# A mixture-of-experts stage: gather and combination as two rounded products with an exact 0/1 table, and the last weight piece loaded during the routing

## The reference

```
aff = softmax(h2 @ w_router)                 # 512 x 16
gval, idx = top_k(aff.T, 64)                 # each expert takes its 64 best tokens
xe  = h2[idx]                                # gather
hid = silu(xe @ w_gate[e]) * (xe @ w_up[e])  # 1024 -> 1024
ye  = (hid @ w_down[e]) * gval
out[idx] += ye                               # combination
```

## Time and profile before

| | us |
|---|---|
| median of 3 timed runs (lowest, highest) | 3082.7 (3081.36, 3086.76) |
| profiled execution | 3083.14 |
| its span, first to last instruction | 3081.3 |
| PE busy | 2980.7 (97%) |
| DVE busy | 1659.1 (54%) |
| ACT busy | 1190.9 (39%) |
| POOL busy | 963.2 (31%) |
| DMA queue q1 | 435.29 MB, 35.9% of 16 engines' span |

### The profile page before, as it was taken

One profiled execution on the slowest core, in us unless ns is written; L12 is line 12 of the kernel. 1 busy time (PEld: TensorE's weight loads), 2 busy tenths in 40 slices (PEclk: granted clock), 3 DMA queues, 4 the chain that ended last, 5 costly groups with the idle time before them and its releaser, 6 DMA issues.

```text
span 3081.3 us, 58082 instructions
## 1 busy us (share of the span) xinstructions
PE 2980.7 (97%) x24214; PEld 2523.1 (82%) x24214; DVE 1659.1 (54%) x2706; ACT 1190.9 (39%) x2273; POOL 963.2 (31%) x685
## 2 busy tenths in 40 slices
PE   7999899999999989999999999999999999999998
PEld 5678788544444449999998999999999999889996
DVE  4257755532212246847384558456676455477583
ACT  3154423110000035535524546346454443364453
POOL 1030367100000024233564432344332366343322
PEclk9999999989999999999999999999999999999999
DMA  7531100359999962322221122222332222113321
GB/s 305 222 129 55 70 3 3 139 214 427 429 429 429 429 264 75 110 83 103 81 99 55 56 97 101 92 103 76 109 110 76 97 83 83 56 69 110 110 78 53
DMA packets 38227, 440.07 MB, mean 143 GB/s; under 512 B 6104, under 2 KB 6744, under 8 KB 11994
## 3 DMA queue, kind: packets, MB, share of 16 engines
q1 hardware_dynamic: 36536, 435.29, 35.9%
q10 hardware_dynamic: 1448, 1.31, 0.1%
HBM read 433.69 MB, written 2.11 MB: 141 GB/s over the span
## 4 chain that ended last, share of the span: by engine, by line
PE 58%; DVE 2%; ACT 2%; issue 1%; POOL 0%; DVEq 0%; ACTq 0%
PE PS L3065 23%; PE PS L2933 23%; PE PS L2930 4%; PE PS L2944 2%; PE PS L3466 2%; PE PS L2521 1%; PE PS L3501 1%; PE PS L2527 1%; PE PS L3484 1%; ACT w_hi L2862 1%; DVE t_lo L3036 0%; ACT h_hi L2743 0%; PE PS L2534 0%; ACT low L2746 0%; PE PS L3461 0%
## 5 line engine op out<-in xcount | busy, mean ns | idle before, releaser
L2875 POOL TENSOR_TENSOR w_lo<-low,w_hi 128x512 fp32r<-128x512 f32 (+4 forms) x310 | 629.0, 2035 | 1522.0 <-ACT w_hi L2862 1517.1
L2862 ACT ACTIVATE w_hi<-low 128x512 fp32r<-128x512 f32 (+3 forms) x670 | 485.3, 743 | 475.4 <-PE PS L2933 290.0
L3065 PE MATMUL PS<-t_hi,w_hi 128*128 128x264 f32 (+1 forms) x1152 | 327.1, 284 | 7.8 <-ACT low L3139 7.8
L3065 PE MATMUL PS<-t_hi,w_lo 128*128 128x264 f32 (+1 forms) x1152 | 327.5, 284 | 0.0
L3065 PE MATMUL PS<-t_lo,w_hi 128*128 128x264 f32 (+1 forms) x1152 | 326.2, 283 | 0.0
L2880 DVE TENSOR_TENSOR w_lo<-low,w_hi 128x512 fp32r<-128x512 f32 x360 | 258.6, 735 | 31.8 <-ACT w_hi L2862 30.5
L3065 PE MATMUL PS<-h_hi,w_lo 128*128 128x264 f32 (+1 forms) x864 | 244.9, 283 | 0.0
L3065 PE MATMUL PS<-h_hi,w_hi 128*128 128x264 f32 (+1 forms) x864 | 244.5, 283 | 0.4 <-issue 0.4
L3065 PE MATMUL PS<-h_lo,w_hi 128*128 128x264 f32 (+1 forms) x864 | 244.8, 283 | 0.0
L2933 PE MATMUL PS<-g_hi,w_hi 128*128 128x264 f32 x1056 | 230.8, 286 | 1.2 <-DVE high L3327 1.2
L2933 PE MATMUL PS<-g_lo,w_hi 128*128 128x264 f32 x1056 | 228.6, 284 | 0.0
(11 more groups left out here) (474 smaller groups left out, 6688.4 us busy)
## 6 DMA issues: line engine op xcount, KB each, us to landing
arena<-wts_dram SPq DMA_DIRECT2D x101, 2048.0 KB, 18.7
low<-wts_dram SPq DMA_DIRECT2D x77, 2048.0 KB, 7.8
arena<-wmod_dram SPq DMA_DIRECT2D x9, 2048.0 KB, 9.0
low<-wts_dram SPq DMA_DIRECT2D x12, 1536.0 KB, 6.4
arena<-na_bias_dram SPq DMA_DIRECT2D x16, 512.0 KB, 3.7
high<-tab_dram SPq DMA_DIRECT2D x1, 2225.0 KB, 25.6
arena<-x_cols_dram SPq DMA_DIRECT2D x1, 2048.0 KB, 8.7
arena<-x_dram SPq DMA_DIRECT2D x1, 2048.0 KB, 8.2
```

Of the source, the lines that this page charges most:

```text
L2862: nc.scalar.activation(hi, raw, ACT.Copy).then_inc(w_h.sem, 1)
L2875: nc.gpsimd.tensor_tensor(lo, raw, hi.bitcast(F32), ALU.subtract).then_inc(w_lp.sem, 1)
L3065: last = nc.tensor.matmul(PS[:, b, 0:n], wt[wi][:, k, :], xs[xi], start=(i in (0, 1, 3) and k == 0 and j == 0), stop=(k == 3 and j == 2), ...
```

## The change

Exact fp32 products with the table are replaced by two rounded ones. A value h is split into h_hi (rounded to fp32r by ACT) and h_lo = h - h_hi (DVE, rounded on writing). The table holds 0 and 1, which fp32r holds exactly, so table x h_hi + table x h_lo gives h up to the rounding of h_lo.

- Gather: `h2` is split in the routing (`split_high` on ACT, `split_low` on DVE). 64 rounded products take the place of 32 fp32 ones. `onehot` is a small rounded table for one pair now, and DVE builds that of the next pair (`next_onehot`) when the gather of the present one is over. The large table (L2280) goes.
- Combination: the table must be 0/1, so the affinity moves into the scaling of `ye`. DVE takes from the transposed weighted table the maximum of each row (`slot_aff`) and the comparison `> 0` (`wcur`, rounded). `ye` is scaled by both `slot_aff` and GT2, ACT rounds it, DVE makes the difference. 16 rounded products take the place of 8 fp32 ones, and four banks (0, 1, 6, 7) take the place of two.
- Last weight piece: the ring gets 95 pieces. Piece 95 (the second half of the last "down") is loaded in two halves of 1 MB into spare room at the end of SP's list of the routing. The DMAs of `meta`, `ln_in` and `final_norm` wait for the last "down", because they write where a half of the piece lies.
- Table 1 is put in another order, so that some of its room is free.

```diff
+            sp.wait_ge(ss_done, TT)
+            sp.wait_ge(h2_done, TT)
+            sp.dma_start(spare[1], last[:, 1, :, :]).then_inc(spare_in, 16)
+            sp.wait_ge(lt_ps, TT)
+            sp.dma_start(spare[0], last[:, 0, :, :]).then_inc(spare_in, 16)
...
+    def split_high(act, n):
+        act.wait_ge(h2_done, n + 1)
+        nc.scalar.activation(h2_hi[:, YORD[n], :], h2[:, YORD[n], :], ACT.Copy).then_inc(hh, 1)
+    def split_low(dve, n):
+        dve.wait_ge(hh, n + 1)
+        dve.wait_ge(ht_ps, 2 * n + 2)
+        nc.vector.tensor_tensor(h2_lo[:, YORD[n], :], h2[:, YORD[n], :], h2_hi[:, YORD[n], :].bitcast(F32), ALU.subtract).then_inc(h_lo, 1)
...
             for n in range(3):          # ACT, routing
                 squares(n)
                 deviation(n)
+                if n == 1:
+                    split_high(act, 0)
+                    split_high(act, 1)
             turned(0)
             turned(1)
+            split_high(act, 2)
...
             turned(3)
+            split_high(act, 3)
             logits(3)
...
             for n in range(TT):         # DVE, routing
                 added(n)
                 normed(n)
+                if n == 2:
+                    split_low(dve, 0)
+                    split_low(dve, 1)
             nc.vector.memset(affT[0:NE, :], 1.0)
+            split_low(dve, 2)
+            split_low(dve, 3)
             dve.wait_ge(lg_ps, 1)
...
+            with sp.Fori(1, NP - 1) as i:
+                load_pair(i, 2 * RING)
+            load_pair(NP - 1, 2 * RING - 1)
...
+            sp.wait_ge(ye_ps, 2 * NP)
             sp.dma_start(res[:, :, 0:NMETA], A["meta"].rearrange("p (k n) -> p k n", k=DK)).then_inc(in_ld, 16)
...
             def gather(i):
                 for k in range(DK):
-                    for t in range(TT):
-                        last = nc.tensor.matmul(..., h2[:, t, k * P:(k + 1) * P],
-                                                onehot[:, t, bass.ds(2 * CAP * i, 2 * CAP)], start=(t == 0), stop=(t == TT - 1))
+                    for x, part in enumerate((h2_hi, h2_lo)):
+                        for t in range(TT):
+                            last = nc.tensor.matmul(..., part[:, t, k * P:(k + 1) * P],
+                                                    onehot[:, t, :], start=(x == 0 and t == 0), stop=(x == 1 and t == TT - 1))
...
             def combine(i):
-                pe.wait_ge(ye_sb, 2 * i + 2)
+                pe.wait_ge(yl_sb, 2 * i + 2)
...
-                    nc.tensor.matmul(PS[:, c % 2, :], wcur[:, t * P:(t + 1) * P], ye[:, half * 512:(half + 1) * 512],
-                                     start=True, stop=True).then_inc(cb_ps, 1)
+                    for x, part in enumerate((ye_hi, ye_lo)):
+                        last = nc.tensor.matmul(PS[:, CBANK[c % 4], :], wcur[:, t * P:(t + 1) * P], part[:, half * 512:(half + 1) * 512],
+                                                start=(x == 0), stop=(x == 1))
+                    last.then_inc(cb_ps, 1)
...
+                for half in range(2):   # ACT, end of pair(i)
+                    act.wait_ge(ye_sb, 2 * i + (half + 1))
+                    nc.scalar.activation(ye_hi[:, lo:hi], ye[:, lo:hi], ACT.Copy).then_inc(yh_sb, 1)
...
             def turned_weights(i):
                 dve.wait_ge(wt_ps, i + 1)
-                nc.vector.tensor_copy(wcur, PS[:, 2, :]).then_inc(wc_sb, 1)
+                nc.vector.reduce_max(slot_aff, PS[:, 2, :], AX.X)
+                nc.vector.tensor_scalar(wcur, PS[:, 2, :], 0.0, None, ALU.is_gt).then_inc(wc_sb, 1)
+                nc.vector.drain()
+            def next_onehot(i):
+                dve.wait_ge(xe_ps, 2 * i + 2)
+                dve.wait_ge(ow_sb, i + 1)
+                for t in range(TT):
+                    last = nc.vector.tensor_tensor(heads(onehot[:, t, :], 2), over(C["iota"], 2), spread(codet[:, t, bass.ds(2 * i + 2, 2)], CAP),
+                                                   ALU.is_equal)
+                last.then_inc(oh_sb, 1)
...
-                    nc.vector.tensor_tensor(ye[:, lo:hi], PS[:, 6 + half, :], GT2[:, lo:hi], ALU.mult).then_inc(ye_sb, 1)
+                    nc.vector.scalar_tensor_tensor(ye[:, lo:hi], PS[:, 6 + half, :], slot_aff, GT2[:, lo:hi], ALU.mult, ALU.mult).then_inc(ye_sb, 1)
+                for half in range(2):
+                    dve.wait_ge(yh_sb, 2 * i + (half + 1))
+                    nc.vector.tensor_tensor(ye_lo[:, lo:hi], ye[:, lo:hi], ye_hi[:, lo:hi].bitcast(F32), ALU.subtract).then_inc(yl_sb, 1)
```

More of the change, by code:

```diff
@@ L2161, in down @@
                         if k % 4 == 0:
-                            w = chunk(i, 8 + 2 * half + k // 4)
+                            if final and half == 1 and k:
+                                pe.wait_ge(spare_in, 32)
+                                w = spare
+                            else:
+                                both = chunk(i, 8 + 2 * half + k // 4)
+                                w = [both[:, j, :, :] for j in range(2)]
                             if half == 0:
@@ L2165, in down @@
                         for j, (a, b) in enumerate(OWN):
-                            last = nc.tensor.matmul(PS[a:b, 6 + half, :], hidT[:, k, j * CAP:(j + 1) * CAP], w[:, j, k % 4, :],
+                            last = nc.tensor.matmul(PS[a:b, 6 + half, :], hidT[:, k, j * CAP:(j + 1) * CAP], w[j][:, k % 4, :],
                                                     start=(k == 0), stop=(k == DK - 1))
@@ L2175, in pair @@
                 gate_up(i, 1)
+                if not isinstance(i, int) or i:
+                    pe.wait_ge(cb_sb, 8 * i + 4)
                 if not last:
-                    if not isinstance(i, int) or i:
-                        pe.wait_ge(cb_sb, 8 * i + 2)
-                    else:
-                        pe.wait_ge(oh_sb, 1)
+                    pe.wait_ge(oh_sb, i + 1)
                     gather(i + 1)
@@ L2183, in pair @@
                 turn_weights(i)
-                down(i)
+                down(i, last)
             gather(0)
@@ L2255, in combined @@
                     x = x1[:, t, half * 512:(half + 1) * 512]
-                    nc.vector.tensor_tensor(x, x, PS[:, c % 2, :], ALU.add).then_inc(cb_sb, 1)
+                    nc.vector.tensor_tensor(x, x, PS[:, CBANK[c % 4], :], ALU.add).then_inc(cb_sb, 1)
             def pair(i, last=False):
                 own_weights(i)
+                if not last:
+                    next_onehot(i)
                 for j in range(2):
@@ L2275, in pair @@
                     lo, hi = half * 512, (half + 1) * 512
-                    nc.vector.tensor_tensor(ye[:, lo:hi], PS[:, 6 + half, :], GT2[:, lo:hi], ALU.mult).then_inc(ye_sb, 1)
-            nc.vector.drain().then_inc(cb_sb, 2)
-            for t in range(TT):
-                last = nc.vector.tensor_tensor(heads(onehot[:, t, 2 * CAP:], NE - 2), over(C["iota"], NE - 2), spread(codet[:, t, 2:], CAP),
-                                               ALU.is_equal)
-            last.then_inc(oh_sb, 1)
+                    nc.vector.scalar_tensor_tensor(ye[:, lo:hi], PS[:, 6 + half, :], slot_aff, GT2[:, lo:hi], ALU.mult, ALU.mult).then_inc(ye_sb, 1)
+                for half in range(2):
+                    dve.wait_ge(yh_sb, 2 * i + (half + 1))
+                    lo, hi = half * 512, (half + 1) * 512
+                    nc.vector.tensor_tensor(ye_lo[:, lo:hi], ye[:, lo:hi], ye_hi[:, lo:hi].bitcast(F32), ALU.subtract).then_inc(yl_sb, 1)
+            nc.vector.drain().then_inc(cb_sb, 4)
             first_rows(0)
```

59 lines of the change are left out of this document (39 added, 20 removed).

## The result

| | before | after |
|---|---|---|
| median of 11 timed runs (lowest, highest) | 3084.33 (3081.36, 3086.76) | 3089.42 (3084.37, 3095.16) |
| ratio after/before, 95% interval | | 1.0019 [1.0011, 1.0026] |
| span of the profiled execution | 3081.3 | 3088.0 |
| code transposes to second block's first matmul | 482.1 | 487.5 |

The kernel became about 5 us slower, against a forecast of 1.9 us faster. The last row is what I compare throughout: it starts at the routing's code transposes (648.13 before, 648.63 after), just ahead of gather(0). Profiles of one kernel against another differ by several us before that point, in the first block, which the change doesn't touch.

The account below looks back on a forecast made before the run. The weight stream (58.8 us a pair at 428 GB/s) was taken to bound the stage. Tail with last piece -1.7 and stream start -0.2 gave -1.9 us: 3083.14 to 3081.2, median 3080.8, stated as 3081.0, range 3077.3 to 3085.

Parts of the forecast that it names:

- Start of the stream (b): gather(0), just ahead of the weight stream: 9.01 us, partly at 1.2 GHz, would get 0.6 us shorter with cheaper records.
- T: The experiments' theory, not the prediction's: loss is PE's clock, left at 1.2 GHz by rounded 128-column records in the first gather.
- rival 1: A rounded 128-column product costs as much as an fp32 one: gather 14.8 us, pairs PE-bound, 3117 us; chance 0.05.
- Rival 4: The clock falls in PE's new gaps inside the stage; two slow pieces in the last pair, 3088 us; chance 0.04.
- Gather: Per pair on PE: 64 rounded records at 0.105 us, 6.9 us in all, 0.5 less than before.
- rival 2: The rounded weight load is faster: gather 4.1 us, gather(0) gains 4.0 instead of 0.6, 3077.6 us; chance 0.05.
- Savings inside the stage worth nothing: In the pairs: PE would need 53.9 us against the stream's 58.8, so it would only wait some 4.9 us more.
- Routing: Ahead of the stream: splitting h2 mostly fits idle time of ACT and DVE, delaying the softmax by 0.4 us.
- Last piece: End of the stream: with one piece preloaded, down ends at 1110.1 instead of 1111.55, a gain of 1.45 us.
- Tail: From down to the second block: 2.2 us scaling and rounding before a faster combination; second block 1.7 us earlier, last piece included.
- rival 3: SP's wait for the last down delays ln_in and final_norm, features(0) at 1139: +15 us, 3098; chance 0.03.
- rival 5: The weight stream is not the bound, so up to 29 us come free in the pairs, 3054 us; chance 0.03.

Follow-up runs that it names:

- cold_wide: wide without the 15 dummy products (results unread) that keep PE at work during the routing's top-64 search; 1.0007 of before, gather(0) 9.9 us.
- nospare: The changed kernel with the last weight piece back in the ring, 96 pieces in the stream; 1.0020 of before.
- cold_narrow: The changed kernel without the 15 dummy products that keep PE at work during the routing's top-64 search; 1.0028 of before, gather(0) 13.8 us.
- t23: The changed kernel with two dummy products of 512 columns ahead of the last combination and three behind it; 1.0013 of before.
- w2: The changed kernel with two fp32 dummy products of 512 columns on PE behind the routing's code transposes; 0.9998 of before, gather(0) 7.3 us.
- slow: w2 with three dummy products of 512 columns on PE behind each pair's combination; 0.9996 of before.
- early: w2 with the first weight piece's products moved between k-tiles 4 and 5 of gather(0); 1.0001 of before.
- wide: The changed kernel with 48 of gather(0)'s 64 rounded products moving 256 columns instead of 128; 0.9998 of before, gather(0) 7.5 us.
- g0: The changed kernel with gather(0) alone as 32 fp32 products of the rounded part, low part left out; 0.9994 of before.
- bw2: The kernel before with the same two dummy products behind the code transposes as w2; 1.0002 of before.
- best1: w2 with the dummy products of t23 around the last combination; 0.9999 of before.
- best2: wide with the dummy products of t23 around the last combination; 0.9995 of before.

## Why the prediction was wrong

**The step that failed** is "Start of the stream (b)": "With 0.105 instead of 0.115 per record, doubled in the slow part, -0.6." It took the slow part of gather(0) as given, as long as it had been (650.6 to 654.0), and only re-priced the records in it. But how long it lasted changed with the records. In after the clock was down for 17 us, from 651.1 to 668.1, over the rest of the gather and on into the first piece. In place of -0.6 the profile showed +4.6 for gather(0) and +1.9 for piece 0; with the routing's 0.5 the stream started 7.0 us later. Two of the prediction's own signs of being wrong came with it: records further than 0.18 us apart (0.212), and a clock under 1.00 inside the stage.

What the clock did with each kind of product, where the profiles show it: it came back during the fp32 gather (before, 3.7 us in) and during the one with 256 columns (cold_wide, 5.3 us in). During the rounded gather with 128 columns it didn't (after, nospare, cold_narrow), and once it fell (t23). The timed runs bear out both comparisons, w2 with after and cold_wide with cold_narrow. The idea behind T, that what counts is for how long columns move behind each load, is not shown: the runs compare two widths only. And the rounded gather doesn't always lose the clock when it starts with it: in w2, slow, early and best1, with the dummies right ahead, it ran at 1.00 to its end.

The prediction's bounds for the record gave "-3.6 and +9.4", and +7.0 lies inside them, but by luck: +9.4 was the price of a rounded record that costs as much as an fp32 one everywhere (rival 1), and at full clock the record cost 0.112.

**Rival 4** was the nearest, "the clock falls", but it looked for that in the gaps that the change opens in the pairs, and priced two slow pieces in the last pair. Those gaps did nothing: up to 1.24 us, clock 1.00 over the whole pair. The 5 us were lost in the densest row of the timeline, and that its 3088 comes near the measured 3089.4 is luck. New gaps did go with a low clock in the tail (2.24 and 2.66 us), which it did not price.

Step by step:

- *Combination* forecast 4.3, was 4.54. *Gather* forecast 6.9, was 7.17 (0.112 a record, not 0.105): right in kind, small misses. Rival 1 (0.232 a record) and rival 2 (0.064) are both refuted. On rival 2 the Trainium skill, "TensorE: Matmul & The Clock Gate", section "Weight-path perf modes — Fast Weight Load (FWL) and DoubleRow", has loads of 128 weights in a type other than FP32 go faster. If rounded fp32 counts as such, the runs disagree: 0.112 us a record, and in wide 1.75 times the columns for 0.24 us more. (The prediction gives what this rule would take off the sum as 3.5 us; its own rival 2 works it out to 3.4.)
- *Savings inside the stage worth nothing*: right, and shown by slow. PE waited 3.3 us a pair, not 4.9. Of the 1.6, 0.5 are the two misses of size above, 0.1 the pair of 58.7 instead of 58.8, and 0.5 that a piece behind a wait takes 3.65 where one in the flow takes 3.47 (839.29 - 825.43 in the earlier trace rows, a quarter of it), three times; the rest I did not follow.
- *Routing* forecast +0.4. The softmax moved from 629.51 to 630.02, but operations at 603 and 618, ahead of the rounding, had moved by the same 0.5, so the rounding itself cost nothing that this profile shows.
- *Last piece* forecast -1.45; nospare shows 1.4 in the stream.
- *Tail*: 2.2 us forecast between down and combination, 2.24 measured. From the end of down to the second block 18.4 were forecast; 18.1 where the clock stayed up (w2, g0, early and the three with dummies in the tail), 19.4 in after, where x1's diagonal products ran at 0.72. That is a second loss of clock, behind a wait on DVE that was 0.30 us and is now 2.66. Six of the nine profiles without dummies there had one in the tail, and neither before nor bw2 did (18.7 and 18.6); that the longer waits are the cause is likely, not shown.
- *New wait on SP*, rival 3: refuted. ln_in's issue took 0.66 us instead of 21.49.
- *Stream the bound*, rival 5: refuted, share 1.01 as before.

So the mechanism of the stage was right, and at full clock its size nearly so: w2 less bw2 is -1.8. That this is so near to -1.9 is in part luck. The forecast holds +0.4 for the routing, which the stages leave out; without it, it was -2.3 (lead -0.6, end of down -1.45, tail -0.25), against -0.1, -1.2 and -0.5 measured. From there to the measured stages: after less w2 is +7.7 in the lead, -0.3 in the stream and +1.3 in the tail, the first and the last from the clock, and bw2 less before is -1.5, before's own loss in the same place. -1.8 + 8.7 - 1.5 = 5.4 = 487.5 - 482.1.

**Open.** Why the clock is up at the start of gather(0) in some profiles (in w2, slow, early, bw2 and best1, all with the two dummies, but also in g0, wide, t23 and best2, with 1.54 us idle as in after) and down in others (before, after, nospare). Within one profile each, I can't say how often either happens; the timed medians say that after lost it often. And why 128 rounded columns behind each load leave the clock low where 256, or fp32 products, do not.

## What to carry to other kernels

Before a product is replaced by narrower or cheaper ones, look at the granted clock where it starts. Here a run of weight loads with 128 rounded columns behind each counted as busy in every row and still stayed at 1.2 GHz, and then the piece behind it paid too. When a transfer stream bounds the middle of a stage, count an engine's saving only in the lead and the tail: here the same change was worth nothing inside the pairs and went with a loss of 6.5 us in the lead. And an earlier start of a stream helps only if the slots behind the first also come free in time: in early the second came 7 us after the first, for a transfer of 4.9.

## What the runs showed of the hardware

- The clock fell with PE busy for 2 us without a break (t23, at 658.7, busy since 656.71), and stayed down through 13.8 us of rounded 128-column records (cold_narrow). With 256 columns in three of four it was back after 5.3 us (cold_wide).
- A rounded 128x128 load and its 128 columns take 0.112 us at 2.4 GHz and 0.213 at 1.2; with mostly 256 columns (wide) 0.117 a record (7.51 / 64, a quarter of them with 128).
- SP's issue of `ln_in` took 21.49 us in before, where PE was still to wait for two of the ring's pieces. It took 4.61 us in nospare and 0.66 in after, in both behind the end of the last down, and in nospare with one more piece in the queue.
